# Branch products of the layers as three rounded products

## The reference

```python
def hybrid_layer(x, ...):
    u = layer_norm(x) * (1 + sc1) + sh1
    proj = u @ w_in + b_in                      # 2564 columns, then 4 x 1024 gate columns
    y_pool = pool_mixer(p_in, w_pool, pool_scale)          # (256 tokens, 256)
    y_conv = short_conv_mixer(c_b, c_c, c_h, conv_w)       # gate_b * conv(gate_c * h)
    y_moba = attention of 4 heads; y_fox = attention of 4 heads with forget sums
    gates = sigmoid(gate_logit)
    merged = sum over n of gates[:, n*1024:(n+1)*1024] * (branches[n] @ w_branch[n])
    x = layer_norm(ALPHA * x + g1 * (merged @ w_o)) * ln1_g + ln1_b
    u2 = layer_norm(x) * (1 + sc2) + sh2
    hdn = square(relu(u2 @ w_up + b_up))
    return layer_norm(ALPHA * x + g2 * (hdn @ w_down)) * ln2_g + ln2_b
```

## Time and profile before

| | us |
|---|---|
| median of 3 executions | 1511.95 |
| lowest, highest | 1504.79, 1512.63 |
| the profiled execution's own time | 1508.91 |
| its span | 1507.1 |
| TensorE busy | 1360.5 (90%) |
| VectorE busy | 963.0 (64%) |
| ScalarE busy | 501.0 (33%) |
| GpSimd busy | 145.6 (10%) |
| mean granted clock of TensorE | 0.955 |

### The profile page before, as it was taken

One profiled execution on the slowest core, in us unless ns is written; L12 is line 12 of the kernel. 1 busy time (PEld: TensorE's weight loads), 2 busy tenths in 40 slices (PEclk: granted clock), 3 DMA queues, 4 the chain that ended last, 5 costly groups with the idle time before them and its releaser, 6 DMA issues.

```text
span 1507.1 us, 18982 instructions
## 1 busy us (share of the span) xinstructions
PE 1360.5 (90%) x7921; PEld 1115.3 (74%) x7921; DVE 963.0 (64%) x1231; ACT 501.0 (33%) x730; POOL 145.6 (10%) x163
## 2 busy tenths in 40 slices
PE   6999997897997888999998899995999999699996
PEld 1688754543795548888996898984988898598995
DVE  3657464753746875676678766667657677755556
ACT  1322134400434503352332433431453323334431
POOL 2011000100100010001222000001001132000000
PEclk9999999999999998998999899997999999899998
DMA  9353350321640057456565666655556476455551
GB/s 335 142 183 111 117 195 0 112 86 54 225 153 1 1 191 249 155 209 246 209 244 195 214 229 230 221 171 189 167 180 252 152 275 238 131 168 195 169 194 56
DMA packets 104918, 257.97 MB, mean 171 GB/s; under 512 B 8217, under 2 KB 11770, under 8 KB 104578
## 3 DMA queue, kind: packets, MB, share of 16 engines
q1 hardware_dynamic: 80554, 171.78, 33.3%
q0 software_dynamic: 20192, 75.58, 13.8%
q10 hardware_dynamic: 4088, 9.41, 1.9%
HBM read 255.70 MB, written 1.05 MB: 170 GB/s over the span
## 4 chain that ended last, share of the span: by engine, by line
PE 74%; DVE 15%; ACT 4%; issue 3%; ACTq 1%; DMA 1%; POOL 1%; SPq 0%; POOLq 0%; DVEq 0%
PE bank L729 72%; PE bank L875 2%; DVE weights_low L1951 2%; DVE modulation_sums L1769 1%; ACT weights_high L1403 1%; DMA x<-in_ctx_dram 1%; POOL inverse_roots L642 1%; ACT odd_prob L1577 1%; DVE statistics L1911 1%; DVE x L2373 1%; DVE even_A L1896 1%; DVE statistics L1809 1%; DVE x L1910 0%; DVE uT_high L2220 0%; DVE odd_weights_low L1951 0%
## 5 line engine op out<-in xcount | busy, mean ns | idle before, releaser
L1951 DVE TENSOR_TENSOR weights_low<-weight_ring,weights_high 128x2048 fp32r<-128x2048 f32 (+1 forms) x128 | 286.1, 2236 | 283.0 <-ACT weights_high L1403 282.9
L1403 ACT ACTIVATE weights_high<-weight_ring 128x2048 fp32r<-128x2048 f32 (+1 forms) x128 | 238.6, 1865 | 528.6 <-PE bank L729 453.9
L729 PE MATMUL bank<-uT_high,weights_high 128*128 128x256 f32 (+1 forms) x1200 | 346.6, 289 | 7.8 <-DVE weights_low L1951 3.0
L729 PE MATMUL bank<-uT_low,weights_high 128*128 128x256 f32 (+1 forms) x1200 | 344.3, 287 | 0.0
L729 PE MATMUL bank<-uT_high,weights_low 128*128 128x256 f32 (+1 forms) x1200 | 343.9, 287 | 0.0
L729 PEld LDWEIGHTS bank<-uT_high,weights_high 128*128 128x128 f32 (+1 forms) x1200 | 233.7, 195 | 12.8 <-issue 10.1
L729 PEld LDWEIGHTS bank<-uT_low,weights_high 128*128 128x128 f32 (+1 forms) x1200 | 233.7, 195 | 1.0
L729 PEld LDWEIGHTS bank<-uT_high,weights_low 128*128 128x128 f32 (+1 forms) x1200 | 233.6, 195 | 0.5
L1769 DVE SCALAR_TENSOR_TENSOR modulation_sums<-modulation_ring,silu_c_columns,modulation_sums 128x1024 f32<-128x1024 f32 x128 | 175.3, 1369 | 9.9 <-DMA modulation_ring<-in_w_ada_dram 6.9
L729 PE MATMUL bank<-weights_high,hidden_high 128*128 128x512 f32 x256 | 101.7, 397 | 5.2 <-DVE weights_low L1951 5.2
L729 PE MATMUL bank<-weights_low,hidden_high 128*128 128x512 f32 x256 | 101.2, 395 | 0.0
(11 more groups left out here) (287 smaller groups left out, 2168.1 us busy)
## 6 DMA issues: line engine op xcount, KB each, us to landing
weight_ring<-in_w_in_dram SPq DMA_DIRECT2D x52, 1024.0 KB, 6.5
modulation_ring<-in_w_ada_dram POOLq DMA_DIRECT2D x48, 1024.0 KB, 7.4
weight_ring<-in_w_up_dram SPq DMA_DIRECT2D x32, 1024.0 KB, 5.3
weight_ring<-in_w_down_dram SPq DMA_DIRECT2D x32, 1024.0 KB, 4.9
modulation_ring<-in_w_mod_dram POOLq DMA_DIRECT2D x16, 1024.0 KB, 5.4
weight_ring<-in_o_w_in_dram SPq DMA_DIRECT2D x10, 1024.0 KB, 5.1
weight_ring<-in_w_branch_dram SPq DMA_DIRECT2D x16, 512.0 KB, 3.6
weight_ring<-in_w_o_dram SPq DMA_DIRECT2D x8, 1024.0 KB, 6.9
```

What stands on the lines that cost most here:

```text
L729: return track(pe.matmul(*args, **kw))
L1403: act.activation(ring[:, s, 0:kn * cols], wring[:, slot, 0:kn * cols], ACT.Copy).then_inc(S["high_ready"], 1)
L1951: dve.tensor_tensor(lo[:, s, 0:kn * cols], wring[:, slot, 0:kn * cols], hi[:, s, 0:kn * cols].bitcast(F32), ALU.subtract).then_inc(w_free[ ...
```

## The change

The branch slabs are cut into parts too. ScalarE's new `high_branch(g)` copies the slab with rounding into a buffer of its own, `branch_weights_high` (128 x 1024, one slot), when TensorE is through with the branch slab before. VectorE's new `low_branch(g)` subtracts it from the slab in place, in the ring's slot (the name `even_weights_low` lies over `weight_ring`). TensorE waits for that (`branch_low`) and makes 24 rounded products a slab where there were 8 in float32. It gives the slot back as before. The branch rows are kept as two parts: the low ones where `yT` was, the high ones over the tile `xn`, in places whose content is no longer needed. VectorE writes both.

```diff
@@ LAYER counts
+    "branch_high": (0, 8), "branch_low": (0, 8), "branch_free": (0, 8),
@@ buffers
+        ylow = sb("branch_rows_low", [P, TALL, D], F32R, where=in_place)
+        yhigh = sb("branch_rows_high", [P, 4, 2, N], F32R, where=in_place)
+        bhigh = sb("branch_weights_high", [P, 2 * COLS], F32R, where=hyb)
-        yT = x[:, TC:TALL, :].rearrange("p t n -> p (t n)").rearrange("p (b m n) -> p b m n", b=4, m=2)
+        ylow = ylow[:, TC:TALL, :].rearrange("p t n -> p (t n)").rearrange("p (b m n) -> p b m n", b=4, m=2)
+        y_at = (0, 3, 1, 2)
+        def branch_view(sec, j):
+            slot = sec.slab((f"branch{j}", 0))[0]
+            return [v.rearrange("p (k n) -> p k n", k=2) for v in (bhigh[:, :], wlow_e[:, slot, 0:2 * COLS])]
@@ TensorE, gate_tile(j)
-                    w = slab(f"branch{j}", 0)
+                    pe.wait_ge(S["branch_low"], sec.at("branch_low", j + 1))
+                    w = branch_view(sec, j)
...
-                                ins = product(o[:, N * m:N * m + N], w[:, k, c:c + P], yT[:, n, k, :],
+                                ins = multiply(o[:, N * m:N * m + N], cut(w, k, c, P),
+                                                [yhigh[:, y_at[n], k, :], ylow[:, n, k, :]],
                                                 start=(k == 0), stop=(k == 1))
                         done(ins, ("prod", j, i))
                     used(ins, f"branch{j}", 0)
+                    signal(ins, S["branch_free"])
@@ ScalarE, loop over g, behind the exponentials
+                def high_branch(j):
+                    slot, before = sec.slab((f"branch{j}", 0))
+                    act.wait_ge(w_full[slot], before * 16 + 16)
+                    if sec.layer > 0 or j > 0:
+                        act.wait_ge(S["branch_free"], sec.at("branch_free", j))
+                    act.activation(bhigh[:, :], wring[:, slot, 0:2 * COLS], ACT.Copy).then_inc(S["branch_high"], 1)
...
+                    high_branch(g)
                     if g < 7:
                         high(f"gate{g + 1}")
@@ VectorE, convolution
-                dve.tensor_tensor(yT[:, 1, :, :], cb, cc[:, :, :], ALU.mult).then_inc(S["conv_ready"], 1)
+                link(dve.tensor_tensor(cc[:, :, :], cb, cc[:, :, :], ALU.mult))
+                link(dve.tensor_copy(yhigh[:, y_at[1], :, :], cc[:, :, :]))
+                dve.tensor_tensor(ylow[:, 1, :, :], cc[:, :, :], yhigh[:, y_at[1], :, :].bitcast(F32), ALU.subtract
+                                  ).then_inc(S["conv_ready"], 1)
@@ VectorE, forget_and_pool
                     o = ready(("mixT",))
+                    hi, lo = yhigh[:, y_at[0], :, :], ylow[:, 0, :, :]
                     for m in range(2):
-                        ins = dve.tensor_scalar(yT[:, 0, m, :], o[:, N * m:N * m + N],
+                        ins = dve.tensor_scalar(hi[:, m, :], o[:, N * m:N * m + N],
                                                 lcol[:, R_PS + m:R_PS + m + 1], None, ALU.mult)
+                    link(ins)
+                    for m in range(2):
+                        ins = dve.scalar_tensor_tensor(out=lo[:, m, :], in0=o[:, N * m:N * m + N],
+                                                       scalar=lcol[:, R_PS + m:R_PS + m + 1],
+                                                       in1=hi[:, m, :].bitcast(F32), op0=ALU.mult, op1=ALU.subtract)
                     release(ins, ("mixT",))
+                def low_branch(j):
+                    slot, _ = sec.slab((f"branch{j}", 0))
+                    dve.wait_ge(S["branch_high"], sec.at("branch_high", j + 1))
+                    dve.tensor_tensor(wlow_e[:, slot, 0:2 * COLS], wring[:, slot, 0:2 * COLS],
+                                      bhigh[:, :].bitcast(F32), ALU.subtract).then_inc(S["branch_low"], 1)
@@ VectorE, loop over g
-                        ins = dve.tensor_copy(yT[:, 2 + a // 2, a % 2, :], o[:, 0:N])
-                        release(ins, ("PV", a))
+                        hi, lo = yhigh[:, y_at[2 + a // 2], a % 2, :], ylow[:, 2 + a // 2, a % 2, :]
+                        link(dve.tensor_copy(hi, o[:, 0:N]))
+                        release(dve.tensor_tensor(lo, o[:, 0:N], hi.bitcast(F32), ALU.subtract), ("PV", a))
+                    low_branch(g)
                     if g < 7:
                         low(f"gate{g + 1}")
```

More of the change, by code:

```diff
@@ L313, in program @@
         acc0 = sb("modulation_sums", [P, 2, D])
+        in_place = ExitStack()
+        ylow = sb("branch_rows_low", [P, TALL, D], F32R, where=in_place)
+        in_place.close()
         x = sb("x", [P, TALL, D])
```

## The result

| | before | after |
|---|---|---|
| median of 20 executions each, us | 1512.88 | 1518.95 |
| lowest, highest | 1504.79, 1517.18 | 1508.83, 1525.65 |
| ratio | | 1.0038, 95% interval 1.0023 to 1.0054 |
| share of full rate granted to TensorE, mean over executions | 0.9518 (60 executions) | 0.9475 (20) |

The changed kernel is 5.7 us slower (0.38%; 3.5 to 8.2). A second comparison on one chip gave 1.0050 (1.0027 to 1.0073). The prediction said 1513.0, range 1502.5 to 1520, and within 0.5% with 0.71. The range held, but the clock, which the sum put at nothing, decided, and in the place and direction of its third rival. Ratios and their intervals leave out one execution of e1 that took 1960.6 us.

A forecast was written before the change was run, and what follows sets the result against it. TensorE was taken as the bound, with 74% of the chain. Tile 0's added wait less the gains at tiles 1 and 2 gave +0.5 us a layer, +1.0 in all: 1511.95 + 1.0 = 1513.0 us, range 1502.5 to 1520.

The forecast's parts named there:

- Rival 3: Tile 0: the longer idle stretch brings a clock fall behind it in each layer, 3.4 us each, 1519.8; chance 0.15.
- The gain on TensorE: Branch slabs: 24 rounded products take 2.88 us instead of 3.45, 0.57 shorter each, 9.1 us over 16 slabs.
- Where it is worth nothing: Behind tiles 3 to 7 TensorE already waits for another engine, so 5.7 us of the 9.1 becomes idle time.
- which the branch products don't touch: Tiles 3 to 7: waits count from the end of the gate products, so 0.57 us saved a slab is idle.
- Tile 0: Branch products wait for VectorE's added rows and slab subtraction: start 2.2 us later, end 1.6 later (1.4 to 1.8).
- The covers: Added ScalarE and VectorE work hides behind existing waits: 16 x 1.0 us of high_branch, low_branch with 1.5 us or more spare.
- the convolution's "Zero": Ahead of the loop: VectorE's extra steps cost TensorE up to 0.9 us, which a later low-part wait takes up; net zero.
- The sum without the clock: Both layers: +1.6 at tile 0, -0.5 at tile 1, -0.57 at tile 2, +0.5 a layer, +1.0 us in all.
- The clock: Tiles 2 and 3: falls to half rate, four times, 3.4 us each; the change was taken to have no net effect.
- Rival 2: Tiles 2 and 3: the clock's falls go away when they begin later, -3.4 us each; chance 0.07 for three or more.
- Rival 4: VectorE late at every tile: subtraction costs 2.29 us, tile 0 loses 1.1 more, 1515.2; within the likeliest case's range.
- Rival 1: All branch slabs: copies and waits hidden, the saving shows in full, -9.1 us, 1502.8; chance 0.07.

The follow-up runs named there:

- e1: Changed kernel with twenty products on constants put into TensorE's wait at tile 0 of each layer; median 1515.19 us, ratio to the kernel before 1.0013.
- e5: Changed kernel with tanh and gated products ahead of the second half of the next gate slab, tiles 0 to 6; 1507.54 us, ratio to before 0.9966.
- e8: Changed kernel with branch slab 0's low part early, plus five products on constants behind the branch products of tiles 4 and 6; 1507.47 us, ratio to before 0.9973.
- e3: Changed kernel with all added work and waits, but eight float32 products a slab, of the high parts only; 1519.92 us, ratio to before 1.0053.
- e2: Changed kernel with branch slab 0's low part and the mixT rows moved ahead of the forget sums; 1513.42 us, ratio to before 1.0000.
- e4: Kernel before with only 24 rounded products a slab, on a constant matrix for the weights, no other work added; 1508.47 us, ratio to before 0.9980.
- e9: Changed kernel, nothing moved, products on constants filling tile 0's wait (twenty) and behind branch products of tiles 4 and 6 (five each); 1507.19 us, ratio to before 0.9968.
- e6: Kernel before with tanh and gated products ahead of the second half of the next gate slab, tiles 0 to 6; 1508.84 us, ratio to before 0.9977.
- e7: Changed kernel with tanh and gated products first, and branch slab 0's low part early; 1499.84 us, ratio to the kernel before 0.9917.
- e10: The changed kernel once more, unaltered, on the same chip as e9; 1520.20 us, ratio to the kernel before 1.0050.

## Why the prediction came out as it did

**The gain on TensorE (right).** 2.83 us a slab for the 2.88 of the sum; 3.45 before.

**Where it is worth nothing (right in kind, wrong by 0.3 a tile).** Tiles 3 to 6 do wait for chains that start near the end of the gate products: e5 shortened them and they moved, and e8's pads cost nothing. But "which the branch products don't touch" failed: the signal that starts the chain rides on the first branch product. Tiles 3 to 6 gained 0.34, 0.30, 0.30 and 0.29 us. e3, with float32 products and all else of the change, has 5.62 at tile 4 again, which shows the cause.

**Tile 0 (right).** Predicted 2.2 us later; from VectorE's mixT step to the first branch product it went from 0.98 (653.98 to 654.96) to 2.98 (665.35 to 668.33), 2.0 later. The rows' and the slab's prices were 0.88 for 0.90 and 1.22 for 1.22.

**The covers (right for the slabs, wrong for the convolution).** high_branch took 1.07 in the mean and low_branch 1.34 (median 1.22), and TensorE waited for a branch slab in no tile but 0. But the convolution's "Zero" failed: it costs 1.2 us a layer. The low part of in3 ended late and TensorE lost 1.02, close to the prediction's "up to 0.9". The step that failed is that a later wait would take this up. The low part waited for there comes at the end of a chain that starts at ScalarE's high part (608.99 before, 620.37 after), and this one waits for TensorE itself, so it moved with the delay: from it to TensorE's next start it is 12.80 us in both kernels.

**The sum without the clock.** Tile 0: +2.0 and 0.6 less for its products (2.9 us to the transposes in e2, e4 and e9, 3.5 before); tiles 1 and 2: 0.6 less each; tiles 3 to 6: 1.2 less. That is -1.0 a layer, -2.1 in all, where the sum had +1.0. With 2.4 for the convolution it is +0.3: the two errors nearly cancel, and that this sum came close is luck.

**The clock (the step that failed).** "I take no net effect for the likeliest case" put at nothing the term that is larger than the rest of the sum. Executions of before spend 145.5 us at half rate in the mean (two times the missing share of the clock, times the span), those of the change 159.4: 13.9 more. Over 60 executions of before a microsecond at half rate goes with 0.48 of time (0.44 over all 80, and 0.44 by the gate products, where a fall of 3.4 us costs 1.5). So this is +6.6 by estimate, or +5.9 with the lower figures. The new sum is -2.1 + 2.4 + 6.6 = +6.9 (+6.2), inside the measured 3.5 to 8.2.

Where this time at half rate lies is shown only in part. The two profiles of the change have five and four new falls of 3.4 us, 15.3 us in the mean; but the falls at tiles 2 and 3 are 6.8 us shorter in all. The loops so have 8.5 us more at half rate, and are 1.7 us longer in the mean of the two profiles (277.2 and 275.8 against 274.8), as -2.1 + 8.5 x 0.44 = +1.6 has it. With 2.4 for the convolution that is 4 of the 5.7 us; the rest is not found there. Behind the second loop the profiles of the change take 245.1 and 243.5 us where before took 242.2, with 31 and 28 us at half rate for 22, though nothing there was changed.

The one profile of before may also have longer loops than most of its executions: e4's and e6's are 8.1 and 7.8 us shorter, their medians only 4.3 and 3.5 us lower. Between kernels with the rounded products, where this doesn't enter, the loops give nearly what the medians give: e1 5.3 us below the mean of the two profiles of the change (median 3.8 below the change), e2 6.2 (5.5), e5 12.6 (11.4), e7 19.5 (19.1), e8 13.6 (11.5). e9 is the exception, 6.8 (11.8).

So the fills show that falls of the clock cost time here and that the kernel is no slower than before without them; how the 5.7 us divide among the places is known to 2.4 for the convolution and stays open for the clock.

Rival 3 had the place and the direction. It asked 3.4 us for a fall and expected one place; a fall costs 1.5, at two kinds of place. The second kind, behind tiles 4 and 6, no rival had: the dense stretch of branch products ahead of the modulation sums got 0.6 us shorter and the thin stretch behind it 0.3 longer (e4 has the falls with no work added, e8's pads, which undo both, take them away). Rival 2 came in part: each layer lost 3.4 of the 13.7 us at half rate at tiles 2 and 3, about 1.5 us of time, where its price was 3.4 for a whole fall. Its premise was loose too: ahead of tile 2's fall TensorE did not only products of 4 rows but also score products of 64 and a mask product of 128. Rival 4 did not come; VectorE was late in no other tile. And the chances of rivals 1 and 2 add up to 0.14, not 0.13.

**Rival 1, the full saving,** is what e7 shows against e6: 9.0 us for the 9.1 of the sum. This agreement is partly luck. The stages give some 3 us a layer, the convolution takes 1.2 of them back, and 13 us less at half rate in the mean (131 against 144) are about 6: some 10 in all. The loops of the two profiles differ by 10.0.

**Still open.** Why e9 lost 29 us of half rate against e10, when its filled places account for about 14: falls elsewhere went too, and no run tells whether by their shift in time. And the time ahead of the first mixT product, most of it in the first network, which the change doesn't touch: 652.9 us in the profile of before, 654.3 in that of e6, 659.3 to 664.3 in the ten others. The clock has most of this: 47.8 and 44.4 us of it at half rate in the first two, 54.6 to 64.9 in the others, so 17.1 us more at 0.44 are 7.5 of the 11.4, and 1.2 are the convolution. It isn't bound to the added work, since e4 has it (662.4), and it doesn't carry to the medians as it stands: e7's profile is 8.4 us longer there than e6's, and its median is 9.0 us lower. But before was profiled once, so no run tells whether a few microseconds of it belong to the change.

## What to carry to other kernels

Shortening or delaying TensorE's work can cost more at the clock than it saves in the stage. So count, for each wait that an edit makes longer and each dense stretch that it makes shorter, what the clock was granted behind it, and if in doubt fill the gap with products on constants and see. A delay is taken up by a later wait only if the chain behind that wait doesn't start from the delayed engine. A signal that is carried by the next instruction makes that instruction's length part of another engine's chain. And a faster stage pays only once the chain beside it is shortened: the same three-part products were 0.4% slower alone and, with two steps put in another order, 0.8% faster than the kernel before, 0.2% of which the new order gives without them (e6).

## What was not expected of the hardware

Products whose results nobody reads made a kernel 13 us faster (1520.2 to 1507.2), of which the loops of the two profiles show 6.0. A full idle of 3.0 us inside a tile brought a fall in 8 of 8 layers, idles of 1.0 to 1.9 us at that place in 0 of 12, and the wait filled with products in 0 of 4. The fall begins 0.8 to 1.6 us behind the restart, so it hits work that is dense again. In the old order, some 2.2 us without dense products behind tiles 4 and 6, with 3.5 us of branch products ahead, left the clock alone (before, e3; in e8 and e9 about 1.9); some 2.5 us with 2.9 us ahead brought 12 falls in 20 places. The two lengths changed together, so no run tells which of them counts.
